# A hybrid decoder trunk on one core: the fourth weight split goes behind the residual adds, tile 0 is added on VectorE, and the first pair of output tiles takes its products of high parts first

## The reference

```python
h = h + 0.5 * _rmsnorm(_swiglu(_rmsnorm(h, g[0, 0]), ffn_w_in[i, 0], ffn_w_out[i, 0]), g[0, 1])
u = _rmsnorm(h, g[1, 0])
# m = mixer(u): stick-breaking attention, latent attention, RWKV-7, stick-breaking attention
h = h + _rmsnorm(m, g[1, 1])
h = h + 0.5 * _rmsnorm(_swiglu(_rmsnorm(h, g[2, 0]), ffn_w_in[i, 1], ffn_w_out[i, 1]), g[2, 1])
```

## Time and profile before

| | |
|---|---|
| median of 3 runs | 2467.89 us (2464.91 to 2468.38) |
| the profiled execution | 2467.77 us, of which 2466.0 us from the first to the last instruction |
| PE busy | 2335.2 us, 95% |
| POOL busy | 1816.6 us, 74% (w_lo, L1263: 1607.9 us) |
| DVE busy | 1475.7 us, 60% |
| ACT busy | 1019.0 us, 41% |
| mean granted TensorE clock | 0.977 |

### The profile page before, as it was taken

One profiled execution on the slowest core, in us unless ns is written; L12 is line 12 of the kernel. 1 busy time (PEld: TensorE's weight loads), 2 busy tenths in 40 slices (PEclk: granted clock), 3 DMA queues, 4 the chain that ended last, 5 costly groups with the idle time before them and its releaser, 6 DMA issues.

```text
span 2466.0 us, 53538 instructions
## 1 busy us (share of the span) xinstructions
PE 2335.2 (95%) x20654; PEld 2259.9 (92%) x20664; DVE 1475.7 (60%) x1834; ACT 1019.0 (41%) x1513; POOL 1816.6 (74%) x853
## 2 busy tenths in 40 slices
PE   7999999999999789999999689989999999999998
PEld 7999989999998789999999578988999999998997
DVE  6972148935963336963981866636982893335982
ACT  4344344344343434344343444324343434444342
POOL 5887737887886607887888796837888788746886
PEclk9999999999999989999999689999999999999999
DMA  5554524554563304564554232013554455433553
GB/s 185 172 193 139 180 65 141 173 201 128 171 196 121 122 10 145 170 198 126 171 189 157 79 112 94 5 37 106 174 185 166 149 180 190 141 108 105 176 187 112
DMA packets 89949, 348.83 MB, mean 141 GB/s; under 512 B 9968, under 2 KB 11760, under 8 KB 89712
## 3 DMA queue, kind: packets, MB, share of 16 engines
q1 hardware_dynamic: 89840, 347.31, 44.1%
HBM read 346.22 MB, written 1.05 MB: 141 GB/s over the span
## 4 chain that ended last, share of the span: by engine, by line
PE 46%; DVE 21%; issue 16%; POOL 8%; ACT 6%; DVEq 1%; DMA 0%; ACTq 0%; SPq 0%; POOLq 0%
PE bank L296 11%; PE bank L298 11%; PE bank L297 11%; DVE hid_hi L1483 8%; DVE hid L1481 6%; POOL w_lo L1263 6%; PE bank L625 3%; ACT sg L978 3%; DVE gs L1424 3%; PE bank L359 2%; DVE hid_lo L1485 1%; PE bank L360 1%; PE bank L361 1%; ACT w_hi L882 1%; POOL h L1276 1%
## 5 line engine op out<-in xcount | busy, mean ns | idle before, releaser
L1263 POOL TENSOR_TENSOR w_lo<-raw,w_hi 128x1024 fp32r<-128x1024 f32 (+2 forms) x608 | 1607.9, 2669 | 568.5 <-ACT w_hi L882 547.2
L296 PE MATMUL bank<-x_hi,w_hi 128*128 128x272 f32 (+1 forms) x3380 | 995.8, 295 | 41.2 <-POOL x_lo L1289 14.9
L298 PE MATMUL bank<-x_hi,w_lo 128*128 128x272 f32 (+1 forms) x3380 | 981.6, 290 | 0.0
L297 PE MATMUL bank<-x_lo,w_hi 128*128 128x272 f32 (+1 forms) x3380 | 978.0, 289 | 0.0
L882 ACT ACTIVATE w_hi<-raw 128x1024 fp32r<-128x1024 f32 (+2 forms) x608 | 660.7, 1115 | 233.8 <-PE bank L298 214.4
L296 PEld LDWEIGHTS bank<-x_hi,w_hi 128*128 128x128 f32 x3380 | 643.2, 190 | 57.8 <-issue 33.7
L297 PEld LDWEIGHTS bank<-x_lo,w_hi 128*128 128x128 f32 x3380 | 644.9, 191 | 0.2
L298 PEld LDWEIGHTS bank<-x_hi,w_lo 128*128 128x128 f32 x3380 | 643.8, 190 | 0.0
L1485 DVE TENSOR_TENSOR hid_lo<-hid,hid_hi 128x272 f32 (+3 forms) x176 | 423.1, 2404 | 20.2
L296 PE MATMUL bank<-hid_hi,w_hi 128*128 128x272 f32 (+1 forms) x1408 | 405.2, 288 | 3.0 <-POOL w_lo L1263 2.9
L298 PE MATMUL bank<-hid_hi,w_lo 128*128 128x272 f32 (+1 forms) x1408 | 403.4, 287 | 0.0
(11 more groups left out here) (277 smaller groups left out, 2325.1 us busy)
## 6 DMA issues: line engine op xcount, KB each, us to landing
raw<-in_ffn_in SPq DMA_DIRECT2D x352, 512.0 KB, 3.5
raw<-in_ffn_out SPq DMA_DIRECT2D x128, 704.0 KB, 4.0
raw<-in_sb_in SPq DMA_DIRECT2D x48, 512.0 KB, 3.6
raw<-in_rw_in SPq DMA_DIRECT2D x24, 512.0 KB, 3.3
raw<-in_sb_out SPq DMA_DIRECT2D x16, 512.0 KB, 3.5
raw<-in_mla_out SPq DMA_DIRECT2D x8, 512.0 KB, 3.3
raw<-in_rw_lora SPq DMA_DIRECT2D x8, 512.0 KB, 4.6
raw<-in_rw_out SPq DMA_DIRECT2D x8, 512.0 KB, 3.3
```

The source lines that it names most:

```text
L296: nc.tensor.matmul(o, wh, xh[:, k, cols()], start=start, stop=False)
L297: nc.tensor.matmul(o, wh, xl[:, k, cols()], start=False, stop=False)
L298: last = nc.tensor.matmul(o, wl, xh[:, k, cols()], start=False, stop=stop)
L1263: nc.gpsimd.tensor_tensor(w_lo[:, s, w], raw[:, s, w], w_hi[:, s, w], ALU.subtract).then_inc(lo_ready, 1)
```

## The change

Five things:

- **The fourth unit.** The split of the next section's fourth unit moves: on ACT from before the inverse root to behind it (`norm_out`), on POOL from before the residual adds to behind them (`add_residual`). This holds for all boundaries but the one into the latent attention (`fourth_unit_late`) and the end.
- **Tile 0.** DVE adds h[0] += m[0] itself, directly behind the first scaling, with a wait on that one; POOL adds tiles 1 to 7.
- **Order of products.** In `first_round` PE takes, for each tile k, w_hi x_hi and w_lo x_hi of units 0 and 1 as soon as x_hi[k] is there, then the block of unit 2 if there is one, then waits for x_lo[k] and takes w_hi x_lo of both units. Unit 2 and unit 3 keep their order.
- **Both units at once.** PE now waits for `w_lo` of units 0 and 1, and for both banks, before the first product.
- **FILL** is 10 in place of 17.

`norm_out` gets the section as a further argument where it is called, and `output_section` takes the place of the call of `split_section` and `add_residual` for each sub-layer's last section (in `time_mixing` on POOL three units are split, then `add_residual` follows); those lines are left out below.

The number of matmuls, but for the fill, of splits and of adds stays the same.

```diff
--- before.py
+++ after.py
@@ -34,7 +34,7 @@
 V_MIX, V_W0, V_KK, V_KA, V_RK, V_LNW, V_LNB = 5, 53, 69, 77, 85, 93, 101
 LAG = 3
 SUM_AFTER = 6
-FILL = 17
+FILL = 10
 NCH, LEVELS = 5, 6
 PAIRS = 4
 NEG = -1e30
@@ -243,6 +243,11 @@
             after = following[sec.name_key]
             body(sec.iters - 1, lambda s: ahead(after, 0, s) if after else None)
 
+        def fourth_unit_late(sec):
+
+            after = following[sec.name_key]
+            return after is not None and after.name != "mla_in"
+
         z_banks = (4, 5, 0, 1)
         following = {s.name_key: t for s, t in zip(secs, secs[1:] + [None])}
 
@@ -257,7 +262,7 @@
         @block.tensor
         def _(pe):
             uses = [0] * 8
-            n = dict(x=0, hid=0, sq=0, head=0, mhead=0, vt=0, hsum=0, kept=0, cut=0)
+            n = dict(x=0, hid=0, sq=0, head=0, mhead=0, vt=0, hsum=0, gained=0, kept=0, cut=0)
             take = iter(secs)
             cols = lambda: slice(n["cut"], L)
 
@@ -343,24 +348,48 @@
 
                 base = n["x"]
                 n["x"] += DT_
-                paced, early = [], DT_ // 2 if behind_norm else 0
-                for k in range(DT_):
-                    paced += [(0, k), (1, k)] + ([(2, k // 2)] if early and k % 2 else [])
-                rest = [(2, k) for k in range(early, DT_)] + [(3, k) for k in range(DT_)]
-                for at, (s, k) in enumerate(paced + rest):
-                    if at == len(paced) + SUM_AFTER and behind_norm:
-                        input_sum(sum_cut)
+                early, c = DT_ // 2 if behind_norm else 0, cols()
+                w_parts = lambda s, k: (bank[s][:, c], w_hi[:, s, P * k:P * k + P], w_lo[:, s, P * k:P * k + P])
+
+                def unit_begins(s):
+                    pe.wait_ge(lo_ready, sec.start + s + 1)
+                    pe.wait_ge(bank_free[s], uses[s] + 1)
+
+                def block_of_unit(s, k):
                     if k == 0:
-                        pe.wait_ge(lo_ready, sec.start + s + 1)
-                        pe.wait_ge(bank_free[s], uses[s] + 1)
-                    if s == 0:
-                        pe.wait_ge(x_ready, base + k + 1)
-                    o, wh, wl = bank[s][:, cols()], w_hi[:, s, P * k:P * k + P], w_lo[:, s, P * k:P * k + P]
-                    nc.tensor.matmul(o, wh, x_hi[:, k, cols()], start=(k == 0), stop=False)
-                    nc.tensor.matmul(o, wh, x_lo[:, k, cols()], start=False, stop=False)
-                    last = nc.tensor.matmul(o, wl, x_hi[:, k, cols()], start=False, stop=(k == DT_ - 1))
+                        unit_begins(s)
+                    o, wh, wl = w_parts(s, k)
+                    nc.tensor.matmul(o, wh, x_hi[:, k, c], start=(k == 0), stop=False)
+                    nc.tensor.matmul(o, wh, x_lo[:, k, c], start=False, stop=False)
+                    last = nc.tensor.matmul(o, wl, x_hi[:, k, c], start=False, stop=(k == DT_ - 1))
                     if k == DT_ - 1:
                         last.then_inc(unit_used, 1)
+
+                unit_begins(0)
+                unit_begins(1)
+                for k in range(DT_):
+                    if behind_norm:
+                        n["gained"] += 1
+                        pe.wait_ge(hg_hi_ready, n["gained"])
+                    else:
+                        pe.wait_ge(x_ready, base + k + 1)
+                    for s in (0, 1):
+                        o, wh, wl = w_parts(s, k)
+                        nc.tensor.matmul(o, wh, x_hi[:, k, c], start=(k == 0), stop=False)
+                        nc.tensor.matmul(o, wl, x_hi[:, k, c], start=False, stop=False)
+                    if early and k % 2:
+                        block_of_unit(2, k // 2)
+                    if behind_norm:
+                        pe.wait_ge(x_ready, base + k + 1)
+                    for s in (0, 1):
+                        o, wh, wl = w_parts(s, k)
+                        last = nc.tensor.matmul(o, wh, x_lo[:, k, c], start=False, stop=(k == DT_ - 1))
+                        if k == DT_ - 1:
+                            last.then_inc(unit_used, 1)
+                for at, (s, k) in enumerate([(2, k) for k in range(early, DT_)] + [(3, k) for k in range(DT_)]):
+                    if at == SUM_AFTER and behind_norm:
+                        input_sum(sum_cut)
+                    block_of_unit(s, k)
 
             def whole(s, j):
                 return s, j, x_parts, j == 0, j == 7
...
@@ -939,11 +969,13 @@
                 act.wait_ge(hsum_done, n["hsum"])
                 inverse_root(xr, 5, D)
 
-            def norm_out(half):
+            def norm_out(sec, half):
                 n["norm"] += 1
                 act.wait_ge(sum_done, n["norm"])
                 n["kept"] += 1
                 inverse_root(bank[4], 4, D, half)
+                if fourth_unit_late(sec):
+                    split_hi(following[sec.name_key], 0, 3)
 
             def squares_of(sec):
 
@@ -957,7 +989,8 @@
                         last = 2 * t + 1 if two else t
                         act.wait_ge(unit_used, sec.start + RING * i + last + 1)
                         square(bank[2 * t if two else t][:, cols()], base + t, base + per * i + t)
-                        ahead(last)
+                        if not (fourth_unit_late(sec) and last == 3 and isinstance(i, int) and i == sec.iters - 1):
+                            ahead(last)
                 rounds(act, sec, body, split_hi)
                 n["sq"] += DT_
 
...
@@ -1268,12 +1301,26 @@
                         ahead(s)
                 rounds(pool, next(take), body, split_lo)
 
-            def add_residual():
-                for k in range(DT_):
+            def output_section():
+
+
+                sec = next(take)
+
+                def body(i, ahead):
+                    for s in range(RING):
+                        if not (fourth_unit_late(sec) and s == 3 and isinstance(i, int) and i == sec.iters - 1):
+                            ahead(s)
+                rounds(pool, sec, body, split_lo)
+                add_residual(sec)
+
+            def add_residual(sec):
+                for k in range(1, DT_):
                     n["apply"] += 1
                     pool.wait_ge(apply_ready, n["apply"])
                     c = slice(n["cut"], L)
                     nc.gpsimd.tensor_tensor(h[:, k, c], h[:, k, c], m[:, k, c], ALU.add).then_inc(h_ready, 1)
+                if fourth_unit_late(sec):
+                    split_lo(following[sec.name_key], 0, 3)
 
             def low_parts(count, k0=0):
                 for k in range(k0, k0 + count):
...
@@ -1456,8 +1501,13 @@
                 dve.wait_ge(bank_free[b], uses_at[sec.name_key][b] + sec.iters + 1)
                 inverse_root()
                 for k in range(DT_):
-                    nc.vector.scalar_tensor_tensor(m[:, k, cols()], m[:, k, cols()], gain(layer, sub, 1, k), bank[4][:, cols()], ALU.mult,
-                                                   ALU.mult).then_inc(apply_ready, 1)
+                    scaled = nc.vector.scalar_tensor_tensor(m[:, k, cols()], m[:, k, cols()], gain(layer, sub, 1, k), bank[4][:, cols()],
+                                                            ALU.mult, ALU.mult)
+                    if k == 0:
+                        steps.link(scaled)
+                        nc.vector.tensor_tensor(h[:, 0, cols()], h[:, 0, cols()], m[:, 0, cols()], ALU.add).then_inc(h_ready, 1)
+                    else:
+                        scaled.then_inc(apply_ready, 1)
                     if then and k >= LAG:
                         low_part(*then, k - LAG)
                 if then:
```

More of the change, by code:

```diff
@@ L485, in latent_attention @@
                 sec, ready = next(take), x_ready_first(last_slot=1)
+                n["gained"] += DT_
                 uses_at["latents"] = list(uses)
@@ L985, in swiglu @@
                 squares_of(sec_out)
-                norm_out(True)
+                norm_out(sec_out, True)
             def take_o(count):
@@ L1038, in stick_breaking @@
                 squares_of(sec_out)
-                norm_out(False)
+                norm_out(sec_out, False)
             def take_tiles(sec, per_unit, dst, every=2):
@@ L1361, in time_mixing @@
                     split_lo(sec_out, 1, s)
-                for s in range(RING):
+                for s in range(3):
                     split_lo(following[sec_out.name_key], 0, s)
+                add_residual(sec_out)
             for s in range(RING):
@@ L1368, in _ @@
                 split_section()
-                split_section()
-                add_residual()
+                output_section()
                 n["cut"] = last_cut(layer)
```

## The result

The changed kernel takes 2487.03 us, the median of 6 runs (2483.76 to 2494.95), against 2466.93 for the kernel before in 6 runs (2464.26 to 2468.61): a ratio of 1.0085, with a 95% interval of 1.007 to 1.010. It is slower by 20 us. The profiled execution took 2487.62 us, its span is 2485.8.

The account below looks back on a forecast made before the run. PE was taken as the bound, busy 95% of the span. Seven boundaries at 0.84 gave 5.9, the other places -0.4: +5.5 on the profiled 2467.77, 2473.3, stated as 2474; range 2464 to 2488.

Parts of the forecast that it names:

- The lock: A POOL instruction and a DVE one with two SBUF operands exclude each other for the whole instruction; first asker goes first.
- I take "loses": At a boundary, DVE's low part 0, asking 0.05 before POOL's add 2, goes second and ends 0.29 after it.
- the forecast's chain: At each of seven boundaries POOL's fourth split delays low parts 6 and 7; input sum 238.4 against 237.58, +0.84.
- the second rival: At boundaries low part 0 precedes add 2, only low part 7 is shut out; input sum +2.0, time 2484; chance 0.30.
- Tile 0 and PE's start: At a boundary h[0], added on DVE, comes near 1.25 us earlier against the root, PE's first product 1.8 earlier.
- Does not help here: At a boundary, high parts first gain nothing: PE's wait for x_lo[6] stands ahead of tile 7's high parts.
- rival 3: PE's stands at boundaries make the clock fall, about 3 us each: 2482, or 2500 at all nine; chance 0.08.
- start: At the kernel's start PE waits for both units, so three matmuls at half clock come later: +0.7 (0 to +0.8).
- end: At the kernel's end one DVE add precedes seven on POOL in place of eight: +0.1.
- last layer's two: Boundaries into the last layer's attention, -0.3 as PE's 1.12 wait goes, and into the last MLP, +0.4 (-0.8 to +0.9).
- The latent attention: At the boundary into it the split stays, and DVE's add of tile 0 runs into it: -0.1 (-0.5 to +0.4).
- RWKV-7: At the boundary into it, without low parts, the first square moves from 1357.74 to 1356.5: -1.2 (-2 to 0).

Follow-up runs that it names:

- the kernel with the halves: Kernel before plus high parts first behind a norm, third unit split sooner, POOL waiting for acc, fourth unit halved ahead of adds, FILL 14: 2467.71 us.
- the repairs: Three edits stacked on high parts first behind a norm: third unit split sooner, 1.0022; POOL waiting for acc, 1.0020; fourth unit in halves, FILL 14, 1.0006.

## Why the prediction was right in direction, and where it failed

- **The lock: right.** Every low part and add into acc that lay under a split at these boundaries ended 0.3 behind it, and the place of the split decides the time (1.0054 with its move alone, 1.0016 with all but its move).
- **The step that failed** is "I take 'loses'" for low part 0 against POOL's add 2. It was asked 0.07 ahead (226.44 against 226.51; I had 0.05) and went first. With that the forecast's chain (low parts 6 and 7 shut out, +0.84) gave way to the second rival's: low part 7 alone shut out, L1461 behind the next split. That rival put the input sum at 239.6; it stands at 239.64, or 239.42 by the clock of the kernel before. It had a chance of 0.30 where the forecast had 0.42. The 2474 was the wrong branch; the measured 2487 is the rival's 2484 and 3 more. It lies 1 us inside the stated range's end of 2488, and single runs lie on both sides of that end (2483.76 to 2494.95): this is luck as much as reckoning. That low part 6 would have been shut out too had low part 0 lost is argued, and no run shows it.
- **Which of the two collisions costs**: the rival's account named both. Letting acc's add go first brings the input sum back to 15.2, so without the second there is none of the 1.85; the first takes 0.5 of what the earlier start and the new order give.
- **Tile 0 and PE's start: right.** h[0] is there 2.76 us behind the squares' last sum, in place of 4.04: 1.28 sooner (1.25 forecast), PE's first product 1.8 sooner (3.46 against 5.28). That a sooner start is worth nothing when the last tile is late: right (first product at 4.04 with FILL 17, the same 17.1).
- **High parts first: wrong in one point.** "Does not help here" holds in the changed kernel (17.0 with the old order, 17.1 with the new one); on the kernel before it is worth 0.67 per boundary at the input sum, of which the MLP sections give 0.45 back.
- **The clock: mixed.** No boundary alike lost its clock in the changed kernel. The last layer's attention did: granted 0.50 from 2143.9 to 2147.3, behind stands of PE of 1.20 and 1.85 us, with PE busy 1.55 of the 3.40 us just before; with FILL 17 it fell there too. So rival 3 held at this one boundary, on top of rival 2. In the kernel with the split put back and FILL 10, three of the boundaries alike lost it (370.0 among them). The fall there cost 1.5 us, half of the 3 that the rival had put. In the latent attention the clock fell at 792.2, 2.3 us behind a stand of 1.76 that the short fill had left; with FILL 17 it fell there too.
- **The other places**: start +0.2 (+0.7 forecast; the three matmuls stand 0.23 apart there, not 0.256), end +0.15 (+0.1), last layer's two +2.35, of which 1.5 with the clock's fall, and +1.41 (-0.3 and +0.4 in the forecast's branch). The latent attention took 6.5 us less (-0.1 forecast), but so it did in every kernel run here: 153.0 to 156.9 us against 159.6 in the profile of before, in which the clock stood at half for 30.7 us of it (20.5 in the one after, 13.7 to 27.3 in the others). So, as far as single profiles can tell, it is the profile of before that was slow there. RWKV-7 was forecast at -1.2. Its first square did come 1.3 sooner, but the section lasted 349.2 us against 340.9, and 340.7 to 346.1 in the other kernels quoted. What sets this stays open: one stand of PE varies between 3.7 and 6.6 us with no edit that explains it, and the half-clock time is the same 71.7 us in both. Of the 8.3 us, 5.4 lie between PE's stand of 3 us at 139 us into the section and its next one above 1.5 us (123.8 us against 118.4); the kernel with tile 0 alone on DVE took as long there (123.6) and lost nothing in time.

## What to carry to other kernels

When instructions of two engines shut each other out, moving a long one off a start moves it onto whatever the other engine does next. List all of the other's instructions that can be shut out (here those with two operands in SBUF, and the cast from SBUF to SBUF) up to the next point at which somebody waits, and count each collision on through to the second and third. A wait that makes the short one on the critical path go first is cheap: it turned 1.0085 into 1.0024, though w_lo came 1 us late in each MLP section for it. Where a few hundredths of a microsecond decide who goes first, give both outcomes a price and don't trust the one that is read closest.

## What the runs showed that was not expected

- Below a tenth of a microsecond the starts in the profile don't tell who goes first. A low part asked 0.06 us ahead of POOL's add lost, one 0.07 ahead won, at all nine boundaries above (226.44 against 225.79 + 0.72 at the first). But one that stood 0.06 ahead won at the changed kernel's boundary into the latent attention. And in the kernel with the halves one 0.08 ahead lost at 1697.2 and took 1.16, where six others, 0.08 to 0.10 ahead, won; that is the boundary with its input sum at 15.3.
- The cast of one operand from SBUF to SBUF is shut out as well: 2.48 us under a split, 0.30 alone.
- The lock is at work in the MLP sections of the kernel before too, of which the prediction says nothing: 160 of the 176 subtractions that make hid_lo take 2.4 us or more, 0.44 alone. PE is not seen to wait for them, but a shift of POOL's splits there moves what it does wait for, as the repairs show.
- A stand of 1.43 us of PE behind a fill of 10 matmuls let the clock fall to 1.2 GHz at three of seven like boundaries in one execution, and not at the other four.
